# Gate and up products of a feed-forward block: activations stationary, or weights stationary and 256 tokens moving

## The reference, cut to what matters

```python
D_MODEL = 2048
SEQ = 256
D_FF = ((8 * D_MODEL // 3 + 255) // 256) * 256     # 5632 = 11 * 512

def _rms(x, g):
    xf = x.astype(jnp.float32)
    y = xf * lax.rsqrt(jnp.mean(xf * xf, axis=-1, keepdims=True) + EPS)
    return (y * g.astype(jnp.float32)).astype(x.dtype)
...
        y = _rms(h, norm_ffn_g[i])
        h = h + (jax.nn.silu(y @ w_gate[i]) * (y @ w_up[i])) @ w_down[i]
```

## Time and profile before

| | |
|---|---|
| median of the runs | 1479.51 us |
| the profiled execution, its span | 1477.7 us |
| PE busy | 1464.4 us, 99% of the span |
| PEld busy | 1213.6 us, 82% |
| DVE, ACT, POOL busy | 851.4, 697.3, 125.7 us |
| gate and up loads, us to landing | 176 of 512 KB, 3.7 |

### The profile page before, as it was taken

One profiled execution on the slowest core, in us unless ns is written; L12 is line 12 of the kernel. 1 busy time (PEld: TensorE's weight loads), 2 busy tenths in 40 slices (PEclk: granted clock), 3 DMA queues, 4 the chain that ended last, 5 costly groups with the idle time before them and its releaser, 6 DMA issues.

```text
span 1477.7 us, 18301 instructions
## 1 busy us (share of the span) xinstructions
PE 1464.4 (99%) x6817; PEld 1213.6 (82%) x6817; DVE 851.4 (58%) x1023; ACT 697.3 (47%) x936; POOL 125.7 (9%) x115
## 2 busy tenths in 40 slices
PE   8999999999999999999999999999999999999998
PEld 6887888888888888888888888888888888888887
DVE  5599966555445554444555544556566666665553
ACT  6443555544444434444433344445555556665432
POOL 2089110000000000000000000000000211100000
PEclk9999999999999999999999999999999999999999
DMA  9655656666665566666655666655566655545562
GB/s 328 199 175 157 195 186 204 190 183 192 190 192 188 186 197 189 193 190 186 187 190 192 197 189 190 192 186 185 171 197 176 210 155 166 164 129 159 173 209 87
DMA packets 140416, 274.19 MB, mean 186 GB/s; under 512 B 8529, under 2 KB 8781, under 8 KB 140216
## 3 DMA queue, kind: packets, MB, share of 16 engines
q1 hardware_dynamic: 138520, 266.48, 57.9%
q0 software_dynamic: 1792, 6.71, 1.5%
q10 hardware_dynamic: 32, 0.01, 0.0%
HBM read 271.02 MB, written 2.15 MB: 185 GB/s over the span
## 4 chain that ended last, share of the span: by engine, by line
PE 93%; DVE 5%; ACT 1%; DMA 0%; issue 0%; DVEq 0%; SPq 0%
PE acc L1185 29%; PE acc L1187 29%; PE acc L1186 29%; PE tp L1202 2%; DVE w_lo L764 2%; DVE tile L808 2%; PE tp L1417 1%; PE sp L1398 1%; PE tp L1212 1%; DMA w_raw<-in_w_in 0%; DVE tile L1064 0%; ACT tile L685 0%; DVE tile L870 0%; ACT w_hi L485 0%; DVE smx L1068 0%
## 5 line engine op out<-in xcount | busy, mean ns | idle before, releaser
L764 DVE TENSOR_TENSOR w_lo<-w_raw,w_hi 128x1024 fp32r<-128x1024 f32 x500 | 613.2, 1228 | 533.4 <-ACT w_hi L485 532.5
L485 ACT ACTIVATE w_hi<-w_raw 128x1024 fp32r<-128x1024 f32 x500 | 529.4, 1061 | 621.4 <-PE acc L1187 617.0
L1185 PE MATMUL acc<-w_lo,yh 128*128 128x512 f32 x1216 | 477.2, 392 | 6.8 <-DVE yl L777 4.2
L1187 PE MATMUL acc<-w_hi,yl 128*128 128x512 f32 x1216 | 474.8, 390 | 0.0
L1186 PE MATMUL acc<-w_hi,yh 128*128 128x512 f32 x1216 | 474.6, 390 | 0.0
L1185 PE MATMUL acc<-w_lo,hh 128*128 128x512 f32 x784 | 310.7, 396 | 0.0
L1187 PE MATMUL acc<-w_hi,hl 128*128 128x512 f32 x784 | 305.8, 390 | 0.0
L1186 PE MATMUL acc<-w_hi,hh 128*128 128x512 f32 x784 | 305.2, 389 | 0.0
L1185 PEld LDWEIGHTS acc<-w_lo,yh 128*128 128x128 f32 x1216 | 229.2, 189 | 55.5 <-DVE yl L777 4.4
L1187 PEld LDWEIGHTS acc<-w_hi,yl 128*128 128x128 f32 x1216 | 229.2, 188 | 48.0
L1186 PEld LDWEIGHTS acc<-w_hi,yh 128*128 128x128 f32 x1216 | 229.3, 189 | 47.0
(11 more groups left out here) (142 smaller groups left out, 557.7 us busy)
## 6 DMA issues: line engine op xcount, KB each, us to landing
w_raw<-in_w_gate SPq DMA_DIRECT2D x88, 512.0 KB, 3.7
w_raw<-in_w_up SPq DMA_DIRECT2D x88, 512.0 KB, 3.7
w_raw<-in_w_down SPq DMA_DIRECT2D x88, 512.0 KB, 4.1
w_raw<-in_swa_w_in SPq DMA_DIRECT2D x72, 512.0 KB, 3.9
w_raw<-in_w_in SPq DMA_DIRECT2D x64, 512.0 KB, 3.8
w_raw<-in_w_out SPq DMA_DIRECT2D x32, 512.0 KB, 4.4
w_raw<-in_w_ple_gate SPq DMA_DIRECT2D x32, 512.0 KB, 4.5
w_raw<-in_swa_w_out SPq DMA_DIRECT2D x32, 512.0 KB, 4.2
```

Of the source, the lines that this page charges most:

```text
L485: act.activation(w_hi[:, s % SPL], w_raw[:, s % RAW], ACT.Copy).then_inc(hi_ready, 1)
L764: dve.tensor_tensor(w_lo[:, s % SPL], w_raw[:, s % RAW], w_hi[:, s % SPL].bitcast(F32), ALU.subtract).then_inc(lo_ready, 1)
L1185: pe.matmul(dst, xh[:, f, tk], w_lo[:, s % SPL, k], start=(f == 0), stop=False)
L1187: last = pe.matmul(dst, xl[:, f, tk], w_hi[:, s % SPL, k], start=False, stop=(f == CK * n - 1))
```

## The change

In the 22 gate and up units the operands trade places: `flipped_chunk` makes a block of the weight, 128 rows by 128 columns, stationary and moves the activations of all 256 tokens (`yh[:, f]`, `yl[:, f]`). A chunk becomes 24 matmuls of 256 columns: two row blocks, four column blocks, three products. The result has the features on the partitions, two column blocks in each of two banks. The hidden values thus come out as the down products want them, and the transposes of `tile1` and what waited for them are gone.

The token scale now lies along the free axis. For the gate it is spread over all partitions once: DVE writes a diagonal of the scales, PE multiplies it by a matrix of ones (256 columns, behind chunk 9 of the first pair), DVE keeps the result as `rf_wide`. DVE's new `gate` multiplies a gate unit by it at chunk 11, and ACT applies SiLU to the result in SBUF. The up unit is multiplied without its scale; `add_resid` of the down units puts that in instead. ACT makes `hh` at chunk 3 and DVE `hl` at chunk 4, from `tile1` whole.

```diff
     _pairs = 4 if _round < 2 else 3
-    UNITS += [(8, "a"), (8, "d")] * _pairs
+    UNITS += [(8, "d"), (8, "d")] * _pairs
...
 H_FFN = len(HALVES)
 HALVES += "xx" * 4
-H_HID = len(HALVES)
-HALVES += "xx" * 11
 H_PLE = len(HALVES)
 HALVES += "xx" * 4
...
+        rf_rows, all_ones, rf_wide = tile[2][:, 0:256], tile[2][:, 256:384], tile[2][:, 512:768]
+
+        def both_banks(u):
+            return [acc[u % 2][b][:].rearrange("p (k n) -> p k n", k=2) for b in range(2)]
+
...
-            rf = rs[:, R_FFN]
-
-            def pair(s, u, lap, kt=None, first=False, fresh=False):
+            def hidden_high(u, kt, lap=ONCE):
+
+                wait_left(act, u + 1, lap)
+                act.activation(hh[:, bass.ds(kt, 4)], feat(1), ACT.Copy).then_inc(hid_hi, 1)
+
+            def gate(u, lap=ONCE):
+
+                wait_left(act, u, lap)
+                act.activation(tile[0][:], tile[0][:], ACT.Silu).then_inc(silu_done, 1)
+
+            def pair(s, u, lap, kt=None, first=False):
...
-                    if kt is not None and c == 5:
-                        high(H_HID, hh[:, bass.ds(kt, 4)], None, lap)
+                    if kt is not None and c == 3:
+                        hidden_high(u - 2, kt, lap)
                     if c == 11:
-                        if first:
-                            act.wait_ge(got, R_FFN + 1)
-                        else:
-                            wait_left(act, u - 1, lap)
-                        take(u, tok(0), ACT.Silu, rf, lap)
+                        gate(u, lap)
...
                 for t in range(T):
                     cols = resid[:, t, CW * j:CW * (j + 1)]
-                    last = dve.tensor_tensor(cols, acc[u % 2][t][:], cols, ALU.add)
+                    if scale is None:
+                        last = dve.tensor_tensor(cols, acc[u % 2][t][:], cols, ALU.add)
+                    else:
+                        last = dve.scalar_tensor_tensor(cols, acc[u % 2][t][:], scale[:, t:t + 1], cols, ALU.mult, ALU.add)
                 last.then_inc(left["d"], 1)
 
...
 
+            def spread_diagonal():
+
+                dve.memset(all_ones, 1.0)
+                dve.wait_ge(got, R_FFN + 1)
+                for t in range(T):
+                    last = dve.tensor_scalar(rf_rows[:, P * t:P * (t + 1)], ident[:], rf[:, t:t + 1], None, ALU.mult)
+                last.then_inc(rf_diag, 1)
+
+            def keep_spread():
+
+                dve.wait_ge(rf_spread, 1)
+                dve.tensor_copy(rf_wide, sp[0][:, 0:256]).then_inc(rf_ready, 1)
+                dve.wait_ge(rf_ready, 1)
+
+            def gate(u, lap=ONCE):
+
+                wait_unit(dve, u, lap)
+                by = rf_wide.unsqueeze(1).to_broadcast([P, 2, 256])
+                for b, half in enumerate(both_banks(u)):
+                    last = dve.tensor_tensor(feat(0)[:, 2 * b:2 * b + 2], half, by, ALU.mult)
+                last.then_inc(left["d"], 1)
+
             def hidden(u, lap=ONCE):
 
-                wait_left(dve, u, lap)
+                dve.wait_ge(silu_done, pairs_before(u) + 1 + lap.pairs)
                 wait_unit(dve, u + 1, lap)
-                for t in range(T):
-                    last = dve.scalar_tensor_tensor(tok(1)[:, t], acc[(u + 1) % 2][t][:], rf[:, t:t + 1],
-                                                    tok(0)[:, t], ALU.mult, ALU.mult)
+                for b, half in enumerate(both_banks(u + 1)):
+                    last = dve.tensor_tensor(feat(1)[:, 2 * b:2 * b + 2], half, feat(0)[:, 2 * b:2 * b + 2], ALU.mult)
                 last.then_inc(left["d"], 1)
 
-            def pair(s, lap, before, half=None, kt=None, first=False):
+            def hidden_low(u, kt, lap=ONCE):
+
+                dve.wait_ge(hid_hi, pairs_before(u) + 1 + lap.pairs)
+                dve.tensor_tensor(hl[:, bass.ds(kt, 4)], feat(1), hh[:, bass.ds(kt, 4)].bitcast(F32),
+                                  ALU.subtract).then_inc(hid_ready, 1)
+
+            def pair(s, u, lap, before, kt=None, first=False):
                 for c in range(16):
                     split(s + c, lap)
                     if c == 3:
@@ -982,38 +1021,44 @@
                     if first and c == 5:
...
+                        keep_spread()
+                    if kt is not None and c == 4:
+                        hidden_low(u - 2, kt, lap)
+                    if c == 11:
+                        gate(u, lap)
...
+            def flipped_chunk(s, u, c, lap=ONCE):
+
+                if c == 0:
+                    wait_left(pe, u - 2, lap)
+                pe.wait_ge(lo_ready, s + 1 + 8 * lap.oct)
+                for k in range(CK):
+                    f = CK * c + k
+                    for b in range(4):
+                        dst, cols = both_banks(u)[b // 2][:, b % 2], slice(P * b, P * (b + 1))
+                        pe.matmul(dst, w_lo[:, s % SPL, k, cols], yh[:, f], start=(f == 0 and b % 2 == 0), stop=False,
+                                  skip_group_check=True)
+                        pe.matmul(dst, w_hi[:, s % SPL, k, cols], yh[:, f], start=False, stop=False, skip_group_check=True)
+                        last = pe.matmul(dst, w_hi[:, s % SPL, k, cols], yl[:, f], start=False, stop=(f == KT - 1),
+                                         skip_group_check=True)
+                last.then_inc(used, 1)
+
...
-            def pair(s, u, lap, half=None, first=False):
+            def pair(s, u, lap, first=False):
                 for c in range(16):
                     if first and c == 6:
                         wait_half_left(pe, H_FFN + 7)
-                    chunk(s + c, u + c // 8, c % 8, yh, yl, lap)
+                    flipped_chunk(s + c, u + c // 8, c % 8, lap)
                     if first and c == 2:
                         wait_left(pe, OUT_UNIT + 3)
                         to_features(H_FFN + 6, resid[:, :, 3 * CW:])
-                    if half is not None and c == 2:
-                        wait_left(pe, u - 1, lap)
-                        to_features(half, tok(1), lap)
+                    if first and c == 9:
+                        pe.wait_ge(rf_diag, 1)
+                        pe.matmul(sp[0][:, 0:256], all_ones, rf_rows, start=True, stop=True).then_inc(rf_spread, 1)
 
             wait_half_left(pe, H_FFN + 5)
             pair(START[FFN_UNIT], FFN_UNIT, ONCE, first=True)
             with pe.Fori(0, 2) as r:
                 with pe.Fori(0, 3) as j:
-                    pair(START[FFN_UNIT + 2], FFN_UNIT + 2, Lap.at(r, j), H_HID)
+                    pair(START[FFN_UNIT + 2], FFN_UNIT + 2, Lap.at(r, j))
                 lap = Lap.at(r)
                 for d in range(4):
                     for c in range(8):
                         if (d, c) == (0, 0):
-                            wait_half_left(pe, H_HID + 5, lap)
+                            pe.wait_ge(hid_ready, 3 + lap.pairs)
                         if (d, c) == (0, 6):
-                            wait_half_left(pe, H_HID + 7, lap)
+                            pe.wait_ge(hid_ready, 4 + lap.pairs)
                         chunk(START[FFN_UNIT + 8 + d] + c, FFN_UNIT + 8 + d, c, hh, hl, lap)
...
-                        if (d, c) == (0, 2):
-                            wait_left(pe, FFN_UNIT + 7, lap)
-                            to_features(H_HID + 6, tok(1), lap)
                 pair(START[FFN_UNIT + 12], FFN_UNIT + 12, lap)
```

More of the change, by code:

```diff
@@ L269, in build @@
         last_sums = sem("last_sums")
+        rf_diag = sem("rf_diag")
+        rf_spread = sem("rf_spread")
+        rf_ready = sem("rf_ready")
+        silu_done = sem("silu_done")
+        hid_hi = sem("hid_hi")
+        hid_ready = sem("hid_ready")
         stored = sem("stored")
@@ L284, in taker, with wait_half_left, wait_half, pairs_before @@
             return "a" if HALVES[h] == "a" else "d"
[L286 to L293, removed]
+        def wait_half_left(eng, h):
+            eng.wait_ge(tp_left[taker(h)], sum(1 for i in range(h + 1) if taker(i) == taker(h)))
+        def wait_half(eng, h):
+            eng.wait_ge(tp_ready, h + 1)
+        def pairs_before(u):
+            return sum((4, 4, 3)[r] for r in range(3) if u >= FFN_UNIT + 12 * (r + 1)) + (u - FFN_UNIT) % 12 // 2
         def hi_count(h):
@@ L637, in _ @@
             with act.Fori(0, 2) as j:
[L638 to L641, removed]
-                        high(H_HID + 16, hh[:, bass.ds(j * 4, 4)], None, lap)
-                    if c == 11:
-                        wait_left(act, base - 1, lap)
-                        take(base, tok(0), ACT.Silu, rf, lap)
+                pair(START[base], base, Lap(2 * j, j, 2 * j), kt=j * 4)
             for d in range(4):
@@ L779, in low, with add_resid @@
                     last.then_inc(tp_left["d"], 1)
-            def add_resid(u, j, lap=ONCE):
+            def add_resid(u, j, lap=ONCE, scale=None):
                 wait_unit(dve, u, lap)
@@ L984, in pair @@
                         request(R_FFN, 16)
```

(21 more changed lines are left out.)

51 lines of the change are left out of this document (21 added, 30 removed).

## The result

| | before | after |
|---|---|---|
| median of the runs | 1479.47 us (4 runs) | 1501.95 us (4 runs, 1500.03 to 1503.10) |
| ratio, 95% interval | 1 | 1.0153 (1.0140 to 1.0165) |
| span of the profiled execution | 1477.7 us | 1501.2 us (its run took 1502.94) |

The forecast was 1475.1 us. The time lies where R1 put it (1500.9), inside the range and on the other side of no change.

The account below looks back on a forecast made before the run. PE, busy 99% of the span, was taken to bound the kernel. Terms -10.0 + 2.3 + 1.8 + 1.0 + 0.5 = -4.4 us gave 1475.1 us against 1479.5; range 1469 to 1503.

Parts of the forecast that it names:

- R1: Rival for gate and up matmuls: 13.3 ns belong to the instruction, 120.0 ns each, 1500.9 us; chance 25 in 100.
- What the flip costs: Step pricing gate and up units: 2112 matmuls of 512 columns become 4224 of 256 at 113.9 ns, +2.3 us.
- (a): Reading of half-clock matmul steps: the surcharge is 1/16 of the columns, so 256 columns take 113.3 ns.
- (b): Reading of matmul records: 225 ns streaming plus 2 between matmuls at 512 columns, so 114.5 ns at 256.
- (c): Reading of gate and up matmuls: all 13.3 ns belong to the instruction, so 256 columns take 120.0 ns.
- The transposes: Term for PE's inner loop: eleven groups of eight transposes at 0.91 us each go, saving 10.0 us.
- PE's lead in instructions: At the outer loop's way back: a lead of 17 instructions shrinks to 1.9 us, so the loss grows 1.8 us.
- R3: Rival: doubled inner-loop code makes its five jumps back dear, 14 to 22 us more, 1489 to 1497; chance 6 in 100.
- The cover on DVE and ACT: In every pair, extra DVE and ACT work stays hidden behind PE, 3.9 us of cover at chunk 3; nothing added.
- R2: Rival: weight load and stream disturb each other, 116 to 118.5 ns a matmul, 1484 to 1495 us; chance 13 in 100.
- R4: Rival: loads alone bind gate and up matmuls, 110 ns each, -14.2 us, 1458.6 us; chance 3 in 100.
- The outer jump: PE's way back in the outer loop: loss of 0.9 us grows by 1.8 to 2.8 us.

Follow-up runs that it names:

- m1: Kernel's work left out, only trains of 40 PE matmuls of varied widths and operands; float32r steps 226.7 ns at 512 columns, 120.0 at 256.
- e4: Kernel before with 66 of its 88 hidden-value transposes left out, hidden values partly stale; 1471.02 us against 1479.23, ratio 0.9943.
- m2: The trains of m1 with other moving widths and stationary column counts; at 256 columns 120.0 ns with 128 stationary, 113.3 to 118.7 with fewer.
- e1: Kernel before with each gate and up matmul cut in two of 256 columns, activations still stationary; 1510.14 us, ratio 1.0211.

## Why the prediction was wrong

**The step that failed** is the choice in "What the flip costs": I took 113.9 ns, the middle of readings (a) and (b), and left (c), 120.0, to a rival. It measured 120.0: +28.1 instead of +2.3. These 25.8 us are nearly the whole error of 27.9 in the span (1501.2 against 1473.3); the rest of the sum came to -4.6 where -6.7 was forecast.
Reading (a) took the missing surcharge at half clock for a sign that it goes by columns. The observation stands, in this kernel too (0.2133 us for 256 columns from 629.88 on), but a cost that vanishes at 1.2 GHz says nothing about how it goes with width; m1 shows it flat from 512 to 256. Reading (b) split the record of float32r at 512 columns into 165 ns and 225 of streaming, the 165 from float32, which has two records a matmul and only 2.5 ns above its 213.3 (m1's line 109: 24 records for 12 matmuls, 215.8 apart). The split fits the record of 283 at 256 columns too, 165 and 118; what failed was to halve the 225, which is reading (a) over again. I argued that both "rest on rows of this width's behaviour in rate" where no row had float32r at any other width; "nothing excludes it" was the honest weight for (c), which moved the sum by 25.8 us, twice all its small terms together. R1 had a quarter of the chance and the correct time to 1.1 us. Its step is measured; its reason, that the 13.3 belong to the instruction, is not shown, since 6.7 of them go with 112, 80, 64 or 32 stationary columns. What they are made of stays open.

**Right.** The transposes: 10.0 us forecast; e4 was 8.2 faster with 66 of 88 gone, 7.3 without the jump's 0.9, which makes 9.7 for all. PE's lead in instructions: matmuls issued before the jump lasted until 625.84, 2.0 us after 623.8, where 1.9 was forecast. R3, dear inner jumps, did not come. The cover on DVE and ACT held in all pairs but the first: at chunk 3 and 4 of a pair both still wait 2.2 and 2.6 us for the other's data without PE waiting once.

```profile
452.51 1.23 DVE L773 TENSOR_TENSOR w_lo<-w_raw,w_hi 128x1024 fp32r<-128x1024 f32 x1 [2.18 <-ACT w_hi L497]
...
450.47 1.06 ACT L620 ACTIVATE hh<-tile 128x1024 f32 x1 [2.60 <-DVE tile L1007]
```

R2 as it was priced fell: the steps are even, 120.0 in the kernel and in m1's train without any other engine at work, not 116 to 118.5 and uneven. Its one row, 0.23 against 0.227, lay within the rounding of the view. Its mechanism is not excluded: a smaller load makes the step at 256 shorter (m1, m2), though not in order. R4 fell: the step of 111.7 is reached only below 256 columns. (Its 110 ns is not the 109.2 that the forecast put beside it; that would give 1455.3, not 1458.6.)

**Mis-sized.** The outer jump: I kept its length of before, 4.2 us, and it took 4.9, so 3.45 idle and not 2.8. The half clock behind it: 26 matmuls, 5.7 us, +2.6, where I took 1.0 of 0 to 1.6; I bounded it by the one other stretch at 512 columns, which was shorter. The first pair: "0.5 + 1.23 is less than the 2.72 that PE then works, so nothing" stopped at the split of chunk 11. Behind it stand, in the rows above, the gate's two reads (338.21, 1.28), ACT's SiLU (339.53), which ACT does before it splits chunk 12 (340.49), and DVE's split (341.56 to 342.8). From the copy at 336.61 that is 6.2 us against the two chunks of 2.88 that PE had: 0.7 us of pause with the edges.

**Luck.** No other term could have saved the sign: with every small term at zero the change costs 28.1 - 10.0 = 18.1 us.

## What to carry to other kernels

Before halving the moving width of a stream of matmuls, count starts, not columns: with float32r at full clock each start of 256 to 512 columns on 128 stationary ones costs 11 to 17 ns beyond its columns here, so twice the matmuls cost 2112 x 13.3 = 28 us, three times what 88 transposes did. Where two readings of the rows differ by less than 7 ns and thousands of instructions hang on them, the one that nothing excludes deserves the larger weight, or a train of 40 instructions that measures it. Where an engine's loop jumps back dearly, try it with somewhat shorter code: 24 instructions fewer in the loop made a jump of 4.2 us one of 0.2. Why just these decide is open.

## What was not expected of the hardware

- float32r matmuls: 226.7 ns at 512 columns, 120.0 at 256, 13.3 above the columns in both, and nothing above them at half clock (0.427 and 0.2133 us). bfloat16: 2.5 above them in both.
- With 112 stationary columns or fewer, a float32r matmul of 256 takes as little as 113.3 ns, but 104 (118.7) and 96 (116.0) take more than 112 and 80 do; open.
- Float32r at 240, 192 and 128 columns: 112.0, 111.7 and 111.7 ns.
- The jump at the end of PE's outer loop: 4183 ns before, 4890 after, 4206 in e1, 209 in e4.
- The granted clock fell to half for 3.4 us a microsecond after the pause of 2.0 us idle (135.2 to 138.6, before), for 6.8 us within the one of 3.3 idle (628.2 to 635.0, after), and not at all around one of 2.6 (e1, 1.00 from 628 to 640); what decides stays open.
